# Waits, clock and tail of a hybrid decoder step: reordered mixers, squares between the routing's steps, three gather banks

## What is computed

```python
for l in range(2):
    h = rmsnorm(x, norm_mix[l])
    q, fx, ix, g, u = split(h @ w_in[l])
    f = lb + (1 - lb) * sigmoid(fx)
    o, S = hgrn2_scan(silu(q), log(f), 1 - f, ix, S0)   # o_t = S_t^T q_t
    o = headnorm(o) * hg_norm * silu(g)
    yp = pool_w @ (trailing_mean(u, windows 2/4/8/16) - u) * pool_scale
    x = x + concat(o, yp) @ w_o[l]
    h = rmsnorm(x, norm_ffn[l])
    x = x + (swiglu(h) if l == 0 else top_2_of_8_experts(h))
y = rmsnorm(x, norm_final)
```

## Time and profile before

| | us |
|---|---|
| median of three executions | 909.86 (909.73 to 911.65) |
| the profiled execution | 908.34 |
| its span | 906.2 |
| TensorE busy in it | 873.1 (96%) |
| VectorE, ScalarE, GpSimd busy | 687.2, 573.3, 172.1 |
| mean granted clock | 0.985 |

### The profile page before, as it was taken

How to read it: one execution, slowest core, us unless ns; L and a number is a source line. 1 busy time by engine, 2 the same in 40 slices (tenths; PEclk the granted TensorE clock), 3 DMA queues, 4 the chain that set the end, 5 groups by cost and what they waited for, 6 DMA issues and landing times.

```text
span 906.2 us, 14828 instructions
## 1 busy us (share of the span) xinstructions
PE 873.1 (96%) x5725; PEld 806.4 (89%) x5725; DVE 687.2 (76%) x812; ACT 573.3 (63%) x692; POOL 172.1 (19%) x151
## 2 busy tenths in 40 slices
PE   6899999999999999999989999999999999999996
PEld 5899999999999999999889888888888888888885
DVE  5876566777765536975685788989898989898964
ACT  6733676554454337536855678787777878787842
POOL 4231155655521120422530000000000000000001
PEclk9989999999999999999989999999999999999999
DMA  8732237555587535323464699999898999898911
GB/s 300 288 125 79 86 98 270 202 174 179 183 323 263 202 116 172 133 93 128 160 247 131 208 405 351 390 339 402 323 417 311 421 316 415 312 414 314 399 64 49
DMA packets 52118, 222.05 MB, mean 245 GB/s; under 512 B 6176, under 2 KB 6304, under 8 KB 51406
## 3 DMA queue, kind: packets, MB, share of 16 engines
q1 hardware_dynamic: 50670, 210.15, 63.2%
q0 software_dynamic: 960, 9.50, 2.7%
q10 hardware_dynamic: 432, 1.64, 0.4%
HBM read 214.25 MB, written 7.47 MB: 245 GB/s over the span
## 4 chain that ended last, share of the span: by engine, by line
PE 88%; DVE 4%; ACT 4%; issue 2%; POOL 1%; DMA 0%; DVEq 0%; POOLq 0%; ACTq 0%
PE bank L1711 40%; PE bank L1417 11%; PE bank L1418 11%; PE bank L1419 11%; PE bank L1448 4%; PE bank L1683 2%; PE bank L1504 2%; PE bank L1567 2%; PE bank L1771 2%; ACT sb_w_hi L554 1%; PE bank L1720 1%; POOL at_square L412 1%; DVE at_decay L1015 1%; ACT at_act_hi L604 0%; DVE at_proj L1027 0%
## 5 line engine op out<-in xcount | busy, mean ns | idle before, releaser
L945 DVE TENSOR_TENSOR sb_w_lo<-sb_raw,sb_w_hi 128x1024 fp32r<-128x1024 f32 (+1 forms) x116 | 169.8, 1465 | 68.7 <-ACT sb_w_hi L554 67.6
L554 ACT ACTIVATE sb_w_hi<-sb_raw 128x1024 fp32r<-128x1024 f32 (+1 forms) x116 | 126.9, 1102 | 132.6 <-PE bank L1419 129.8
L1417 PE MATMUL bank<-at_act_hi,sb_w_hi 128*128 128x264 f32 x672 | 195.1, 290 | 11.7 <-DVE sb_w_lo L945 8.3
L1711 PE MATMUL bank<-sb_w_hi,at_packed 128*128 128x512 f32 (+1 forms) x768 | 192.1, 379 | 0.0
L1418 PE MATMUL bank<-at_act_lo,sb_w_hi 128*128 128x264 f32 x672 | 192.0, 286 | 0.0
L1419 PE MATMUL bank<-at_act_hi,sb_w_lo 128*128 128x264 f32 x672 | 191.8, 285 | 0.0
L992 DVE TENSOR_TENSOR sb_w_lo<-at_raw_e,sb_w_hi 128x1408 fp32r<-128x1408 f32 (+1 forms) x112 | 159.1, 1446 | 26.6 <-ACT sb_w_hi L621 25.4
L992 DVE TENSOR_TENSOR sb_w_lo<-sb_raw,sb_w_hi 128x1408 fp32r<-128x1408 f32 (+1 forms) x104 | 150.3, 1479 | 18.4 <-ACT sb_w_hi L621 18.4
L621 ACT ACTIVATE sb_w_hi<-at_raw_e 128x1408 fp32r<-128x1408 f32 (+1 forms) x112 | 139.3, 1244 | 36.8 <-PE bank L1711 36.5
L1711 PEld LDWEIGHTS bank<-sb_w_hi,at_packed 128*128 128x128 f32 x768 | 140.3, 189 | 22.5
L621 ACT ACTIVATE sb_w_hi<-sb_raw 128x1408 fp32r<-128x1408 f32 (+1 forms) x104 | 130.5, 1262 | 35.5 <-PE bank L1711 34.7
(11 more groups left out here) (260 smaller groups left out, 1373.2 us busy)
## 6 DMA issues: line engine op xcount, KB each, us to landing
sb_raw<-in_moe_w_up_dram SPq DMA_DIRECT2D x36, 704.0 KB, 7.2
at_raw_e<-in_moe_w_down_dram SPq DMA_DIRECT2D x49, 512.0 KB, 6.2
at_raw_e<-in_moe_w_gate_dram SPq DMA_DIRECT2D x35, 704.0 KB, 8.6
sb_raw<-in_up_units_dram SPq DMA_DIRECT2D x44, 512.0 KB, 3.4
sb_raw<-in_moe_w_gate_dram SPq DMA_DIRECT2D x29, 704.0 KB, 8.3
sb_raw<-in_in_units_dram SPq DMA_DIRECT2D x39, 512.0 KB, 3.4
sb_raw<-in_moe_w_down_dram SPq DMA_DIRECT2D x39, 512.0 KB, 5.1
at_raw_e<-in_moe_w_up_dram SPq DMA_DIRECT2D x28, 704.0 KB, 6.0
```

Of the source, the lines that this page charges most:

```text
L554: act.activation(w_hi[s][:, 0:kts, :], raw[s][:, 0:kts, :], ACT.Copy).then_inc(hi_done, 1)
L945: dve.tensor_tensor(w_lo[s][:, 0:kts, :], raw[s][:, 0:kts, :], w_hi[s][:, 0:kts, :].bitcast(f32), ALU.subtract).then_inc(lo_done, 1)
L1417: pe.matmul(out[:, 0:T], w_hi[s][:, k, :], hi[:, c, :], start=(c == 0), stop=False)
L1711: mm = pe.matmul(bank[first_bank + p][:, 0:width], s, w[:, c0:c0 + width], start=(k == 0 and n == 0), stop=(k == last and n == 2))
```

## The change

On TensorE, `sum_past` of layer 0 stands one unit later, without that of layer 1 waiting for a read; units of layer 0's third group wait for the read of their own bank. One sample head stands in each of (3, 0), (3, 1), (4, 0), (4, 1). In the out passes the first two heads' products of units 0 and 1 alternate. The first units of ffn_up0 and in1 wait tile by tile. The squares' sum is cut in pieces, `sum_m`: two tiles ahead of the placing, four after the counts, two after the first two gathers, in bank 3, and the gathers use three banks; two gathers now follow each of units 0 to 6. The counts wait for the slots, the first gather for its token tiles' marks one by one; gather 2 waits for the longest count. On ScalarE the first table (logarithm) is loaded ahead of all else, the logarithm of the forget gate stands at (1, 1), the copy of the sample sums behind the end decays, and the squares are taken before the third and fourth token tiles are rounded. On VectorE the forget gate stands at (1, 0), the scan at (1, 2), the windows and pooled inputs at (4, 1), and the head scalings alternate with the rests. In the tail TensorE sums the squares into three columns of tokens, root and reciprocal work on 88 x 3, TensorE spreads the result into bank 1 by three products with the identity, and VectorE multiplies in four pieces, sent by SyncE and ScalarE in turn. The order of the gate computations moves by one unit.

```diff
@@ -283,7 +283,7 @@
-GATHERS = {-1: (0, 1), 0: (2,), 1: (3, 4), 2: (5, 6), 3: (7, 8), 4: (9, 10), 5: (11, 12), 6: (13, 14), 7: (15,)}
+GATHERS = {j: (2 * j + 2, 2 * j + 3) for j in range(-1, KT - 1)}
@@ -292,7 +292,7 @@
-    return (3, 4, 6, 7)[n % 4]
+    return (4, 6, 7)[n % 3]
@@ -395,10 +395,10 @@
-    for c in range(2):
+    for c in (0, 2):
...
-        sp.dma_start(o["y"][:, 4 * c:4 * (c + 1), :], y_cols[:, 4 * c:4 * (c + 1), :]).then_inc(y_out, 16)
-    sp.wait_ge(y_out, 16 * 2)
+        sp.dma_start(o["y"][:, 2 * c:2 * (c + 1), :], y_cols[:, 2 * c:2 * (c + 1), :]).then_inc(y_out, 16)
+    sp.wait_ge(y_out, 16 * 4)
@@ -545,6 +545,7 @@
+    act.preload_act_table(ACT.Ln)
@@ -605,7 +606,8 @@
-        act.preload_act_table(ACT.Ln)
+        if nth:
+            act.preload_act_table(ACT.Ln)
@@ -645,9 +647,10 @@
-            if (it, s) == (1, 2):
+            if (it, s) == (1, 1):
...
+            if (it, s) == (1, 2):
@@ -662,14 +665,14 @@
-                act.wait_ge(sampled, 5 * (L + 1))
-                act.activation(sample_sums[:, :, :, :].rearrange("p a h b -> p (a h b)"), bank[2][:, SIDE.start:BESIDE.stop], ACT.Copy).then_inc(sums_copied, 1)
...
+                act.wait_ge(sampled, 5 * (L + 1))
+                act.activation(sample_sums[:, :, :, :].rearrange("p a h b -> p (a h b)"), bank[2][:, SIDE.start:BESIDE.stop], ACT.Copy).then_inc(sums_copied, 1)
@@ -808,13 +811,15 @@
-    for n in range(2, 6):
+    act.wait_ge(bank_read, LAST_UNIT - 1)
+    act.activation(square_m[:, 0:KT - 1, :], xT[:, 0:KT - 1, :], ACT.Square).then_inc(x_squared, 1)
+    round_tokens(2)
+    act.wait_ge(bank_read, LAST_UNIT)
+    act.activation(square_m[:, KT - 1, :], xT[:, KT - 1, :], ACT.Square).then_inc(x_squared, 1)
+    for n in range(3, 6):
...
-    act.wait_ge(bank_read, LAST_UNIT)
-    for c in range(0, KT, 4):
-        act.activation(square_m[:, c:c + 4, :], xT[:, c:c + 4, :], ACT.Square).then_inc(x_squared, 1)
@@ -853,12 +858,12 @@
-        if at == 2:
-            inverse_root(3, 5)
+        if at == 1:
+            inverse_root(3, 3)
...
-        if at == 5:
+        if at == 4:
@@ -907,7 +912,10 @@
-    act.activation(root[:, :], bank[0][:, 0:T], ACT.Sqrt, scale=1.0 / D_MODEL, bias=eps[:, :]).then_inc(rooted, 1)
+    act.activation(root[0:ROWS, 0:3], bank[0][0:ROWS, 0:3], ACT.Sqrt, scale=1.0 / D_MODEL, bias=eps[0:ROWS, :]).then_inc(rooted, 1)
+    for c in (1, 3):
+        act.wait_ge(y_done, c + 1)
+        act.dma_start(o["y"][:, 2 * c:2 * (c + 1), :], y_cols[:, 2 * c:2 * (c + 1), :]).then_inc(y_out, 16)
@@ -1003,23 +1011,11 @@
-            if (it, s) == (1, 1):
-                dve.wait_ge(lb_step, 11)
-                dve.wait_ge(sig_done, L + 1)
-                for h in range(HEADS):
-                    dve.tensor_scalar(proj[:, 1, h, :], proj[:, 1, h, :], lspan[:, L, h:h + 1], lbound[:, L, h:h + 1],
-                                      ALU.mult, ALU.add).then_inc(forget_done, 1)
-            if (it, s) == (1, 3):
+            if (it, s) == (1, 2):
...
-            if (it, s) == (4, 3):
-                dve.wait_ge(windowed, 8 * (L + 1))
-                for g in range(4):
-                    w = (win_a, win_b)[g % 2]
-                    dve.wait_ge(past_added, 4 * L + g + 1)
-                    dve.scalar_tensor_tensor(w[:, g, PAD:], w[:, g, PAD:], 1.0 / WINDOWS[g], up[:, g, PAD:], ALU.mult, ALU.subtract).then_inc(pooled, 1)
@@ -1027,17 +1023,23 @@
+            if (it, s) == (1, 0):
+                dve.wait_ge(lb_step, 11)
+                dve.wait_ge(sig_done, L + 1)
+                for h in range(HEADS):
+                    dve.tensor_scalar(proj[:, 1, h, :], proj[:, 1, h, :], lspan[:, L, h:h + 1], lbound[:, L, h:h + 1],
+                                      ALU.mult, ALU.add).then_inc(forget_done, 1)
...
-            if it == 4 and s < 3:
+            if it == 4 and s < 2:
...
-                for j in ((0,), (1, 2), (3,))[s]:
+                for j in ((0,), (1, 2, 3))[s]:
@@ -1045,7 +1047,7 @@
-            if (it, s) == (4, 2):
+            if (it, s) == (4, 1):
@@ -1054,6 +1056,11 @@
+                dve.wait_ge(windowed, 8 * (L + 1))
+                for g in range(4):
+                    w = (win_a, win_b)[g % 2]
+                    dve.wait_ge(past_added, 4 * L + g + 1)
+                    dve.scalar_tensor_tensor(w[:, g, PAD:], w[:, g, PAD:], 1.0 / WINDOWS[g], up[:, g, PAD:], ALU.mult, ALU.subtract).then_inc(pooled, 1)
@@ -1118,9 +1125,12 @@
+        def scale_head(h):
+            dve.tensor_tensor(hg_tmp[:, h, :], hg_tmp[:, h, :], hg_rstd[:, h, :], ALU.mult).then_inc(hgo_scaled, 1)
+        scale_head(0)
...
-            dve.tensor_tensor(hg_tmp[:, h, :], hg_tmp[:, h, :], hg_rstd[:, h, :], ALU.mult).then_inc(hgo_scaled, 1)
-        for h in range(HEADS):
+            if h + 1 < HEADS:
+                scale_head(h + 1)
@@ -1379,12 +1389,12 @@
-    dve.reciprocal(rstd[:, :], root[:, :]).then_inc(rstd_done, 1)
-    dve.wait_ge(rstd_done, 5)
+    dve.reciprocal(rstd_tok[0:ROWS, :], root[0:ROWS, 0:3]).then_inc(rstd_done, 1)
...
-    for c in range(2):
-        half = slice(4 * c, 4 * (c + 1))
-        dve.tensor_tensor(y_cols[:, half, :], scaled_f[:, half, :], rstd[:, :].unsqueeze(1).broadcast_to([128, 4, T]), ALU.mult).then_inc(y_done, 1)
+    dve.wait_ge(summed, 6)
+    for c in range(4):
+        part = slice(2 * c, 2 * (c + 1))
+        dve.tensor_tensor(y_cols[:, part, :], scaled_f[:, part, :], bank[1][:, 0:T].unsqueeze(1).broadcast_to([128, 2, T]), ALU.mult).then_inc(y_done, 1)
@@ -1407,7 +1417,7 @@
-                    pe.wait_ge(bank_read, n - 4 + halves)
+                    pe.wait_ge(bank_read, n - 7 if n0 == 0 and isinstance(it, int) and it == 2 else n - 4 + halves)
@@ -1432,8 +1442,6 @@
-        if L:
-            pe.wait_ge(norm_lo, KT * 3)
@@ -1468,16 +1476,15 @@
-        SAMPLE_HEADS = {(3, 0): (0, 1), (4, 0): (2, 3)}
+        SAMPLE_HEAD = {(3, 0): 0, (3, 1): 1, (4, 0): 2, (4, 1): 3}
...
-            if (it, s) == (2, 0):
+            if (it, s) == (2, 1 - L):
...
-            if (it, s) in SAMPLE_HEADS:
+            if (it, s) in SAMPLE_HEAD:
...
-                for h in SAMPLE_HEADS[(it, s)]:
-                    sample_head(h)
-            if (it, s) == (4, 0):
+                sample_head(SAMPLE_HEAD[(it, s)])
+            if (it, s) == (4, 1):
@@ -1489,7 +1496,8 @@
-            pe.wait_ge(bank_read, IN0[L] + 8)
+            if L == 0:
+                pe.wait_ge(bank_read, IN0[L] + 8)
@@ -1515,7 +1523,7 @@
-            weight_pass("in1", act_hi, act_lo, part=(0, 1), between=sums_beside)
+            weight_pass("in1", act_hi, act_lo, part=(0, 1), between=sums_beside, operand=lambda c: pe.wait_ge(norm_lo, 2 * KT + c + 1))
@@ -1561,7 +1569,7 @@
-                if s == 0 and k < HEADS:
+                if s < 2 and k < HEADS:
@@ -1629,8 +1637,11 @@
+        for k in range(2):
+            out_part(0, (k,))
+            out_part(1, (k,))
...
-            out_part(s, range(HEADS)).then_inc(unit_used, 1)
+            out_part(s, range(2, HEADS) if s < 2 else range(HEADS)).then_inc(unit_used, 1)
@@ -1641,17 +1652,24 @@
-            pe.wait_ge(norm_lo, KT * 2)
...
-            weight_pass("ffn_up0", act_hi, act_lo, part=(0, 1), between=sums_beside)
+            weight_pass("ffn_up0", act_hi, act_lo, part=(0, 1), between=sums_beside, operand=lambda c: pe.wait_ge(norm_lo, KT + c + 1))
...
+    def sum_m(kts):
...
+        for kt in kts:
+            pe.wait_ge(x_squared, KT // 2 + (1 if kt < KT - 1 else 2))
+            mm = pe.matmul(bank[3][:, 0:T], ones, square_m[:, kt, :], start=(kt == 0), stop=(kt == KT - 1))
+        return mm
...
+    sum_m(range(2))
@@ -1661,24 +1679,28 @@
-    pe.wait_ge(hot, 3)
...
+        pe.wait_ge(route, CHOSEN + 1)
...
+    sum_m(range(2, 6))
...
-        if n == 3:
+        if n == 2:
...
-        if n >= 4:
-            pe.wait_ge(packed_lo, n - 3)
-        pe.wait_ge(hot, min(3 * (q + 1), 9))
+        if n >= 3:
+            pe.wait_ge(packed_lo, n - 2)
+        if n:
+            pe.wait_ge(hot, min(3 * (q + 1), 9))
...
+                if n == 0:
+                    pe.wait_ge(hot, i + 1)
@@ -1723,25 +1745,21 @@
+    sum_m(range(6, KT)).then_inc(summed, 1)
...
-            pe.wait_ge(packed_lo, 14)
+            pe.wait_ge(packed_lo, 16)
...
-        if j == 2:
-            for kt in range(KT):
-                pe.wait_ge(x_squared, KT // 2 + kt // 4 + 1)
-                mm = pe.matmul(bank[5][:, 0:T], ones, square_m[:, kt, :], start=(kt == 0), stop=(kt == KT - 1))
-            mm.then_inc(summed, 1)
...
-        if j == 4:
+        if j == 3:
@@ -1818,10 +1836,15 @@
-    pe.matmul(bank[0][:, 0:T], ones, square_f[:, 0, :], start=True, stop=False)
-    for kt in range(KT - 2, KT):
+    for kt in (0, KT - 2, KT - 1):
...
-        mm = pe.matmul(bank[0][:, 0:T], ones, square_f[:, kt, :], start=False, stop=(kt == KT - 1))
+        for i, (t0, rows) in enumerate(TOKEN_TILES):
```

(10 more changed lines are left out.)

## The result

The median of four executions is 888.53 us (886.84 to 888.86) against 909.97 for the kernel before (909.73 to 911.65): a ratio of 0.9757, 95% interval 0.974 to 0.9774. The profiled execution took 886.84 us, its span is 884.7, TensorE is busy for 863.3 us (98%), and the mean granted clock is 0.998, where it was 0.985.

What follows compares the result with a forecast made beforehand. TensorE was taken as the bound, by waits and by clock falls. Gains of 3.9 + 7.0 + 0.5 + 1.0 + 3.4 + 1.4 + 4.8 + 1.5 + 0.1 = 23.6 us from the median 909.86 gave 886.3, range 881.0 to 896.0.

Steps and rivals of the forecast that it cites:

- the range's lower end: 881.0 us: no stall at level 0 1.0, none in the routing 1.2, tail's upper end 0.8, one fall fewer 1.5.
- Bound: Whole kernel: TensorE bounds it, through its waits and through clock falls that lose 12.2 us in five stretches.
- Past sums of layer 0: Layer 0 mixer: removing the wait for unit 7's read and the fall behind it gains 3.9 us, a 1.0 stall remaining.
- above 2 us: Sign of being wrong: a new TensorE wait on at_sided in layer 0 above 2 us.
- Heads: Mixers' sample heads: one per step instead of pairs removes three clock falls, 7.0 us (0 to 7.0).
- Operands: ffn_up0 and in1: waiting tile by tile covers two waits of 1.7 us for the last normalised tile, 3.4 us.
- Pooling and projection: Both layers: pooled windows a step earlier gain 0.5 us, scalings interleaved with rests in the output projection 1.0.
- Routing: Routing before the experts: squares fill two gaps and keep the clock up, less new waits: 4.8 us; 1.3 if it falls.
- Tail: Kernel's end: reciprocal and root on three columns, less an added broadcast: 1.5 us (0.5 to 2.3).
- Moved falls: Rival, 0.17: heads or the routing's short products still bring the clock down at as many places; 896.7 us.
- VectorE as the bound of the mixers: Rival, 0.08: splits, sides and copies on VectorE pace the score steps, giving 18 us back; 904.3 us.
- serial gathers: Rival, 0.04: with three banks, evictions can't overlap the next unit, costing 33.6 us in the experts' gathers; 919.9 us.

Runs made afterwards that it cites:

- single heads alone: The kernel before with one sample head per step and the copy of the sample sums behind the end decays, nothing else of the change: 905.17 us.
- late squares: The changed kernel with all eight square products of the routing behind the first two gathers: 889.27 us.
- four banks: The changed kernel with a fourth gather bank, so that gather 3 instead of gather 2 waits for the longest count: 888.46 us.
- whole operands: The changed kernel with the first units of ffn_up0 and in1 waiting for all eight normalised tiles again: 891.00 us.
- the fastest one's sister: The 883.18 us kernel (changed kernel plus earlier level 0 steps, routing edits and a fourth gather bank) with three gather banks again: 885.28 us.

## Why the prediction was right

The forecast of 886.3 us stands against 888.53; 21.5 us were gained in the profiled executions where 23.6 were summed, and 21.4 between the medians. The terms named for the range's lower end add up to 4.5 us, which gives 881.8 and not 881.0; nothing hangs on it here.

- *Bound.* TensorE was the bound in both of the ways named, by waits and by clock, and the two were worth about the same: 11.6 us of the gain are falls that went (1.8 behind the gap of layer 0, 6.4 at the heads, 3.4 in the routing), the other 10 are waits and the tail.
- *Past sums of layer 0: the step that failed, in size.* I had moved the q gate by the 2.87 us for which ScalarE idled, "since that wait is for a read queued behind the moved forget gate and scan". Moving the scan ahead of the split of unit 10 put that split beside the differences, and the read behind both: the scan came 3.5 us forward, the q gate 0.4. The stall was 2.0 and not 1.0, just short of the "above 2 us" that I had named as a sign of being wrong; level 0 itself ran 0.3 longer, and 2.5 were gained and not 3.9. The trace of before held the price: its split beside the differences, at 40.33, also took 2.82 us.
- *Heads.* 6.4 of 7.0, and the mechanism is shown from both sides: pairs bring the falls back, singles alone take them away. A single head had no fall behind it in any of the ten profiles with single heads. What I had not seen is that the gaps' falls are not fixed, which made the kernel with single heads alone dearer than 903 to 904.
- *Operands.* 3.9 for 3.4, both 2.0 where the list of waits says 1.7.
- *Pooling and projection.* 1.2 for 1.5: layer 0 0.3 more, layer 1 0.5 less, as its first tile for the routing came late behind a split (0.9 us of wait).
- *Routing.* 4.7 for 4.8, and each part of the sum is in the trace: 0.8 + 1.8 + 3.4 less 0.7 (slots) and 0.6 (longest). I had argued that the squares in the gaps hold the clock; in the one profile without them half of it stayed away, and what kept that half away is open. With the squares in the gaps none of nine profiles has a fall behind the choice and the marks; without them the three (before, single heads alone, late squares) lose 3.4, 3.4 and 1.7 us there.
- *Tail.* 1.3 for 1.5; from the reciprocal's end to the first y product the spread took 1.1, where 0.8 was summed.
- *Rivals.* Moved falls: there is one behind the new stall of layer 0, seen in the profile with four banks, whose code is the changed kernel's up to there. It is the likely reason why the median is 1.7 above the profiled execution, whose clock is 0.998 against 0.995 and 0.996 in the other three; no profile of the changed kernel shows it. The Trainium skill, TensorE: Matmul & The Clock Gate, section "Part 1: The HAM clock gate", says that the window runs free of the kernel; that the same code has the fall in one profile (four banks) and lacks it in four others (the changed kernel, its repeat, late squares, whole operands) agrees. VectorE as the bound of the mixers showed once, at level 0, and nowhere else. Three banks cost 0.6 in the changed kernel, 1.0 in the fastest one's sister, and no serial gathers.

## What to carry to other kernels

Where the granted clock falls behind short products and gaps, as TensorE's did here, a list of waits is half the account: read the granted clock by stretches, and put work that fills the array between short products and into gaps. When a chain is moved earlier, move it on paper with every instruction that stands between its links on each queue, with the duration that it has beside its new neighbours. And a fall that went may wait behind the next gap, so close the largest remaining gap even where it is cheap by itself.

## What had not been expected of the hardware

- Splits on VectorE and differences on GpSimd take turns: 2.82 and 2.57 us for splits of 1.22, and 2.87 for the second of two differences, of which the first took 1.9.
- TensorE is shown as busy for 20.00 of 20 us in stretches where the clock falls (0.91 from 60 us with pairs): products of one column keep it issuing, and the clock falls all the same.
- The clock's fall in the tail comes at another point in each execution: 0.90 to 1.58 us for the same six products.
- A fall behind one and the same gap is not of one length: 3.4 and 6.8 us at half clock behind the 3.1 us gap of layer 0, with the same instructions up to it.
